# First loads of a streaming encoder: x tiles 0 to 2 by ScalarE's queue, norm rows in one transfer, small tables behind x, a third place for turned tiles

## The reference

```
for layer in (0, 1):
    h = rms_norm(x, pre_mix_g[layer])
    y = even_mixer(h) if layer == 0 else gla_mixer(h)
    x = x + rms_norm(y, post_mix_g[layer])
    h = rms_norm(x, pre_ffn_g[layer])
    x = x + rms_norm((silu(h @ w_gate) * (h @ w_up)) @ w_down, post_ffn_g[layer])
```

## Time and profile before

| what | before |
|---|---|
| median of the runs | 1456.67 us (1454.84 to 1458.1) |
| profiled execution | 1451.34 us, its span 1449.5 us |
| busy share: TensorE, VectorE, ScalarE, GpSimd | 96%, 57%, 37%, 27% |
| mean granted TensorE clock | 0.989 of 2.4 GHz |
| moved by DMA | 131.49 MB, mean 91 GB/s |

### The profile page before, as it was taken

One profiled execution on the slowest core, in us unless ns is written; L12 is line 12 of the kernel. 1 busy time (PEld: TensorE's weight loads), 2 busy tenths in 40 slices (PEclk: granted clock), 3 DMA queues, 4 the chain that ended last, 5 costly groups with the idle time before them and its releaser, 6 DMA issues.

```text
span 1449.5 us, 20838 instructions
## 1 busy us (share of the span) xinstructions
PE 1384.4 (96%) x9097; PEld 1313.3 (91%) x9097; DVE 823.7 (57%) x928; ACT 530.4 (37%) x740; POOL 390.2 (27%) x307
## 2 busy tenths in 40 slices
PE   5999989999999999988999999998999999999996
PEld 5998979999999999987899877997979898999996
DVE  4447376765655556458343454647686565555744
ACT  5223243442433334334333213424344243433444
POOL 2042051433324233114001100005143332424304
PEclk9999999999999999988999999999999999999998
DMA  6221204122122212322232321420412212222231
GB/s 213 88 88 45 88 29 160 59 87 89 59 88 88 88 59 87 123 89 102 88 124 81 110 94 59 151 83 30 160 58 88 88 59 91 84 88 87 88 117 73
DMA packets 92144, 131.49 MB, mean 91 GB/s; under 512 B 2631, under 2 KB 76179, under 8 KB 91286
## 3 DMA queue, kind: packets, MB, share of 16 engines
q1 hardware_dynamic: 87832, 110.21, 23.3%
q0 software_dynamic: 3808, 19.42, 3.8%
q10 hardware_dynamic: 414, 0.54, 0.1%
HBM read 114.42 MB, written 15.74 MB: 90 GB/s over the span
## 4 chain that ended last, share of the span: by engine, by line
PE 77%; DVE 13%; ACT 4%; issue 3%; POOL 2%; DMA 1%; ACTq 0%; SPq 0%; DVEq 0%; POOLq 0%
PE ps L550 25%; PE ps L541 19%; PE ps L631 5%; PE ps L586 5%; PE ps L1053 4%; PE ps L798 4%; PE ps L783 4%; PE ps L741 4%; DVE wl L1114 2%; PE ps L666 1%; DVE wl L1249 1%; PE ps L683 1%; PE ps L1026 1%; POOL x L2094 1%; PE ps L1039 1%
## 5 line engine op out<-in xcount | busy, mean ns | idle before, releaser
L1114 DVE TENSOR_TENSOR wl<-stage,wh 128x2048 fp32r<-128x2048 f32 x57 | 140.3, 2462 | 79.5 <-ACT wh L1734 44.5
L1725 ACT ACTIVATE wh<-stage 128x2048 fp32r<-128x2048 f32 x47 | 89.7, 1907 | 179.3 <-PE ps L541 119.8
L2164 POOL TENSOR_TENSOR wsum<-stage 128x512 f32<-128x512 f32 x36 | 46.7, 1296 | 401.8 <-DVE wl L1249 250.5
L1249 DVE TENSOR_TENSOR wl<-wsum,wh 128x2048 fp32r<-128x2048 f32 x36 | 82.5, 2290 | 30.1 <-ACT wh L1754 29.8
L541 PE MATMUL ps<-xh,wh 128*128 128x320 f32 x352 | 80.5, 310 | 3.9 <-DVE qk L1120 2.4
L1803 ACT ACTIVATE gate<-ps 128x320 f32<-128x320 f32 x72 | 31.3, 435 | 143.0 <-PE ps L550 143.0
L1242 DVE TENSOR_TENSOR wbl<-stage,wbh 128x1024 fp32r<-128x1024 f32 x36 | 44.4, 1233 | 67.0 <-ACT wbh L1744 67.0
L541 PE MATMUL ps<-xh,wl 128*128 128x320 f32 x352 | 80.2, 309 | 0.0
L541 PE MATMUL ps<-xl,wh 128*128 128x320 f32 x352 | 80.1, 309 | 0.0
L586 PE MATMUL ps<-wh,xh 128*128 128x256 f32 x240 | 68.1, 284 | 0.0
L586 PE MATMUL ps<-wh,xl 128*128 128x256 f32 x240 | 67.9, 283 | 0.0
(11 more groups left out here) (365 smaller groups left out, 4485.4 us busy)
## 6 DMA issues: line engine op xcount, KB each, us to landing
stage<-w_ffn_gate SPq DMA_DIRECT2D x22, 1024.0 KB, 5.3
stage<-w_ffn_up SPq DMA_DIRECT2D x22, 1024.0 KB, 5.3
stage<-w_ffn_down SPq DMA_DIRECT2D x22, 1024.0 KB, 5.1
stage<-w_in_odd SPq DMA_DIRECT2D x12, 1024.0 KB, 5.3
x_spill<-x POOLq DMA_DIRECT2D x3, 2560.0 KB, 8.5
x<-x_spill SPq DMA_DIRECT2D x3, 2560.0 KB, 10.5
stage<-w_in_even SPq DMA_DIRECT2D x6, 1024.0 KB, 5.0
stage<-w_out_even SPq DMA_DIRECT2D x4, 1024.0 KB, 5.5
```

The costliest lines, as they stand in the source:

```text
L1114: dve.tensor_tensor(wl[:, s].rearrange("p k c -> p (k c)"), stage[:, s, :], f32(wh[:, s].rearrange("p k c -> p (k c)")), ALU.subtract).the ...
L1249: dve.tensor_tensor(wsl[:, u % 2, :], wsum[:].rearrange("p i c -> p (i c)"), f32(wsh[:, u % 2, :]), ALU.subtract).then_inc(w_lo, 1)
L1725: act.activation(wsh[:, u % 2, :], flat_stage(u), ACT.Copy).then_inc(w_hi, 1)
```

## The change

The norm rows are put together on the host into one array of 76 rows of 128 and come in one transfer. ScalarE's own queue issues x tiles 0, 1 and 2 as its first instructions; SP issues the identity, the rows, weight unit 0, x tiles 3 and 4, then weight unit 1. GpSimd waits until x tile 4 has landed before it issues its 13 small loads. Turned tile 2 gets a place of its own, banks 1 and 3 (free until the second half of unit 0); tiles 3 and 4 then wait for tiles 0 and 1 only, and the second half of unit 0 waits until tile 2 has been copied. VectorE's and ScalarE's orders are written out: VectorE gain 0, gain 1, low 0, gain 2, low 1, low 2, gain 3, `lo(0)`, gain 4, low 3, low 4; ScalarE high 0, copy 0, high 1, copy 1, high 2, `hi(0)`, copy 2 (in two halves), then high and copy of tiles 3 and 4.

```diff
+        def x0_banks(t):
+            b = (4, 6, 0, 4, 6)[t]
+            return ps[:, 0:4, :].rearrange("p (i b) n -> p i b n", b=2)[:, :, 1, :] if t == 2 else ps[:, b:b + 2, :]
+        def x0_tiles(t):
+            return x0_banks(t).rearrange("p b (k n) -> p b k n", n=P)
...
-            r0 = 0
-            for name in ("pre_mix_g", "post_mix_g", "pre_ffn_g", "post_ffn_g", "pool_scale", "g_onorm"):
-                src = a[name].rearrange("l (k p) -> (l k) p", p=P)
-                sp.dma_start(rows[r0:r0 + src.shape[0], :], src).then_inc(rows_loads, 16)
-                r0 += src.shape[0]
-            for t in range(TT):
-                src = a["x_prompt"][0, tile(t), :] if t < 4 else a["x_sample"].rearrange("b s d -> (b s) d")
-                sp.dma_start(xin[:, t, :], src).then_inc(x_load[t], 16)
-                if t == 0:
-                    load(0, a["w_in_even"][0, :, 0:UW], wait=False)
+            sp.dma_start(rows[0:ROWS, :], a["rows"]).then_inc(rows_loads, 16)
+            load(0, a["w_in_even"][0, :, 0:UW], wait=False)
+            sp.dma_start(xin[:, 3, :], a["x_prompt"][0, tile(3), :]).then_inc(x_load[3], 16)
+            sp.dma_start(xin[:, 4, :], a["x_sample"].rearrange("b s d -> (b s) d")).then_inc(x_load[4], 16)
...
                 pe.wait_ge(x_load[t], 16)
-                if t >= 2:
-                    pe.wait_ge(x0_done, t - 1)
-                    pe.wait_ge(xg_done, t - 1)
+                if t >= 3:
+                    pe.wait_ge(x0_done, t - 2)
+                    pe.wait_ge(xg_done, t - 2)
                 for k in range(KB):
-                    last = pe.transpose(span(4 + 2 * (t % 2), D)[:, tile(k)], xin[:, t, tile(k)], ident)
+                    last = pe.transpose(x0_tiles(t)[:, k // 4, k % 4, :], xin[:, t, tile(k)], ident)
...
             pe.wait_ge(x0_lo, TT)
+            pe.wait_ge(x0_done, 3)
             first_unit(1).then_inc(w_used, 1)
...
+            x0_gained(0)
+            x0_gained(1)
+            x0_low(0)
+            x0_gained(2)
+            x0_low(1)
+            x0_low(2)
+            x0_gained(3)
+            lo(0)
+            x0_gained(4)
+            x0_low(3)
             x0_low(TT - 1)
...
+            for t in range(3):
+                act.dma_start(xin[:, t, :], a["x_prompt"][0, tile(t), :]).then_inc(x_load[t], 16)
...
+                if t == 2:
+                    for b in range(2):
+                        last = act.activation(x[:, 4 * b:4 * b + 4, tile(t)], x0_tiles(t)[:, b], ACT.Copy)
+                    last.then_inc(x0_done, 1)
...
+            x0_high(0)
+            x0_copy(0)
+            x0_high(1)
+            x0_copy(1)
+            x0_high(2)
+            hi(0)
+            for t in range(2, TT):
+                if t > 2:
+                    x0_high(t)
+                x0_copy(t)
...
+            pool.wait_ge(x_load[4], 16)
             pool.dma_start(cst[:, P:], a["consts"][:, P:]).then_inc(small_loads, 16)
```

More of the change, by code:

```diff
@@ L484, in _ @@
             sp.dma_start(ident, a["consts"][:, 0:P]).then_inc(ident_load, 16)
-            r0 = 0
-            for name in ("pre_mix_g", "post_mix_g", "pre_ffn_g", "post_ffn_g", "pool_scale", "g_onorm"):
-                src = a[name].rearrange("l (k p) -> (l k) p", p=P)
-                sp.dma_start(rows[r0:r0 + src.shape[0], :], src).then_inc(rows_loads, 16)
-                r0 += src.shape[0]
-            assert r0 == ROWS
-            for t in range(TT):
-                src = a["x_prompt"][0, tile(t), :] if t < 4 else a["x_sample"].rearrange("b s d -> (b s) d")
-                sp.dma_start(xin[:, t, :], src).then_inc(x_load[t], 16)
-                if t == 0:
-                    load(0, a["w_in_even"][0, :, 0:UW], wait=False)
+            sp.dma_start(rows[0:ROWS, :], a["rows"]).then_inc(rows_loads, 16)
+            load(0, a["w_in_even"][0, :, 0:UW], wait=False)
+            sp.dma_start(xin[:, 3, :], a["x_prompt"][0, tile(3), :]).then_inc(x_load[3], 16)
+            sp.dma_start(xin[:, 4, :], a["x_sample"].rearrange("b s d -> (b s) d")).then_inc(x_load[4], 16)
             for u in range(1, U_OUT0):
@@ L822, in _ @@
             pe.wait_ge(ident_load, 16)
-            pe.wait_ge(rows_loads, 16 * 6)
+            pe.wait_ge(rows_loads, 16)
             pe.transpose(ps[:, 0, 0:ROWS], rows[0:ROWS, :], ident[0:ROWS, 0:ROWS]).then_inc(rows_full, 1)
@@ L1480, in x0_low, with x0_gained @@
                 dve.tensor_tensor(xl[:, :, tile(t)], xg[:, t % 2], f32(xh[:, :, tile(t)]), ALU.subtract).then_inc(x0_lo, 1)
-            for t in range(TT):
+            def x0_gained(t):
                 dve.wait_ge(x0_full, t + 1)
@@ L1485, in _ @@
                     dve.wait_ge(x0_lo, t - 1)
[L1486 to L1491, removed]
+                dve.tensor_tensor(xg[:, t % 2].rearrange("p (b k) n -> p b k n", b=2), x0_tiles(t),
+                                  gains[:, PRE_MIX:PRE_MIX + KB].rearrange("p (b k) -> p b k", b=2).unsqueeze(3).broadcast_to([P, 2, 4, P]), ALU.mult).then_inc(xg_done, 1)
+            x0_gained(0)
[8 more added lines that the diff above has]
+            x0_low(3)
             x0_low(TT - 1)
@@ L1926, in last_ffn, with x0_high, x0_copy @@
                 first_columns(TT - 1)
-            for t in range(TT):
+            for t in range(3):
+                act.dma_start(xin[:, t, :], a["x_prompt"][0, tile(t), :]).then_inc(x_load[t], 16)
+            def x0_high(t):
                 act.wait_ge(xg_done, t + 1)
                 act.activation(xh[:, :, tile(t)], xg[:, t % 2], ACT.Copy).then_inc(x0_hi, 1)
+            def x0_copy(t):
                 act.wait_ge(x0_full, t + 1)
-                act.activation(x[:, :, tile(t)], span(4 + 2 * (t % 2), D).rearrange("p (k n) -> p k n", n=P), ACT.Copy).then_inc(x0_done, 1)
-                if t == 0:
-                    hi(0)
+                if t == 2:
+                    for b in range(2):
+                        last = act.activation(x[:, 4 * b:4 * b + 4, tile(t)], x0_tiles(t)[:, b], ACT.Copy)
+                    last.then_inc(x0_done, 1)
+                else:
+                    act.activation(x[:, :, tile(t)].rearrange("p (b k) n -> p b k n", b=2), x0_tiles(t), ACT.Copy).then_inc(x0_done, 1)
+            x0_high(0)
[8 more added lines that the diff above has]
+                x0_copy(t)
             for t in range(TT):
@@ L2270 @@
     arrays["consts"] = constants()
+    arrays["rows"] = np.concatenate([arrays[name].reshape(-1, P) for name in ("pre_mix_g", "post_mix_g", "pre_ffn_g", "post_ffn_g", "pool_scale", "g_onorm")])
     aps = {name: nc.dram_tensor(name, x.shape, mybir.dt.from_np(x.dtype), kind="ExternalInput").ap() for name, x in arrays.items()}
```

## The result

| what | before | after |
|---|---|---|
| median of six runs each | 1457.38 us (1454.84 to 1460.04) | 1444.76 us (1442.83 to 1446.89) |
| ratio, 95% interval | | 0.9915 [0.9899, 0.9931] |
| profiled execution, its span | 1451.34, 1449.5 us | 1442.83, 1440.3 us |
| unit 1 starts (profiled execution) | 40.01 us | 31.94 us |

The changed kernel is 12.4 us faster by the ratio, where 7.0 was forecast; 1444.76 lies under the forecast range. The direction and the place were right, the size was not. Between the two profiled executions the span differs by 9.2 us and the start of unit 1 by 8.07.

What follows compares the result with a forecast made beforehand. TensorE, 96% busy, bounds the kernel; unit 1's start hangs on x tile 2. Landing at 10.3, plus 6.8, plus 15.87 puts unit 1 at 33.0 instead of 40.01: 7.0 us off 1456.67 gives 1449.7 us, range 1446.0 to 1454.0.

Steps and rivals of the forecast that it cites:

- How the numbers follow: Whole kernel: 7.0 us comes off the profiled execution (1451.34 to 1444.3) and off the median alike (1456.67 to 1449.7).
- Issue order on ScalarE: Kernel start: ScalarE's DMA issues go ahead of the table load, at 0.75, 1.2 and 1.65 us.
- Tile 2 lands at L = 10.3: First loads: x shares bandwidth half each with SP's queue, so x tile 2 lands at 10.3 us, called L.
- x gets more than half: Rival, 12%, first loads: tile 2 lands at 7.8, unit 1 starts at 30.4, gain 9.6 us, 1447.1 us.
- Unit 0 at L + 6.2, unit 1 at L + 22.7: First product: unit 0 can start 6.2 us after tile 2 lands, unit 1 22.7 after, at 33.0.
- From lo(0) to unit 1, 15.87: VectorE's low part of the weights to unit 1: 15.87 us, kept as one unchanged term.
- TensorE ready 1.1 before unit 1: Ahead of unit 1: TensorE is ready at 31.9 us, so the norm chain still ends last, by 1.1.
- GpSimd's wait costs nothing: GpSimd's 13 issues after tile 4 end at 21.2; its norm power, wanted at 28.7, has 7.5 us of cover.
- GpSimd held by VectorE: Part of a 17% rival: GpSimd's issues wait for busy VectorE, end at 31.5, power 2.8 late, gain 4.2, 1452.5 us.
- Only the issue time is won: Rival, 8%, first loads: tile 2 lands at 14.4, unit 1 starts at 37.1, gain 2.9 us, 1453.8 us.
- Slower by the array's rate: Rival, 5%, unit 0 on TensorE: half rate costs 2.35 us more per pass; with all six, 1462.7 us.
- Cost nothing, cover little: Norm rows in one transfer: there by 5.6 us, 4.4 after issue as upper bound, needed at about 6.6.

Runs made afterwards that it cites:

- before_again: The kernel before, unchanged, run again: 1456.46 us (12 runs); unit 1 at 42.36 us in its profiled execution.
- after_again: The changed kernel, unchanged, run again: 1444.73 us (6 runs), ratio 0.9918 to the kernel before; unit 1 at 31.66 us.
- after_late: The changed kernel with 80 unread products of the tile of ones between unit 0 and unit 1 on TensorE: 1459.70 us.
- before_c: The kernel before, unchanged, run for one more profiled execution: unit 1 at 42.10 us, 1410.0 us from there to the end.

## Why the prediction came out too small

**The step that failed** is in "How the numbers follow": "the sum is of differences inside the span, so it goes off either". It took 40.01 us, the start of unit 1 in one execution, as the kernel's own, and so also L = 17.36 for tile 2. That execution took 1451.34 us where the runs' median was 1456.67; I noted the distance and did not ask where it lay. About 2.4 us of it lay in the stretch that the change removes: typical is 42.4 (the median of the six is 42.35).

**The sum with what was measured.** Forecast 7.0; the new start 1.1 earlier than forecast (31.9 for 33.0); the old start 2.4 later: 10.5. The spans of the profiled executions say the same (means 1452.5 of six and 1442.0 of three, 10.5). The medians differ by 11.6 to 12.6, the means of all runs with a clock on record by 11.2, runs at equal clock by 10.4 to 11.6. So about 1 us between the starts and the runs stays open, no more than the uncertainty: the mean of six starts of before is itself known to 0.9 to either side. A smaller share of half-rate time in the changed kernel, which I had expected for the rest, is not needed and not shown: runs at or under 0.984 are 27 of 70 before and 3 of 13 after, and the difference stays when the clock is equal.

**The new start, by its steps.**
- *Issue order on ScalarE*: right. DMA issues at 0.75, table load at 2.15 behind them.
- *Tile 2 lands at L = 10.3*: too late, it landed at 8.6. Half each against the weights was right: 0.62 MB against 0.56 from 5.2 to 8.3, with three packets of SP for one of x, not one for one. Mis-sized was the time that x has alone. SP's queue held the identity and the rows ahead of the weight unit, 204 packets of 512 B; from 3.5 to 5.0 x moved 0.57 MB of 0.61. I had counted 0.33 MB ahead of the sharing. The rival "x gets more than half" gave L = 7.8 and a start of 30.4 for another reason; neither L nor start was reached. Tiles 3 and 4 came at 12.0 and 13.3, some 0.5 later than forecast, so the turns were not back to back; turn 3 waited 1.81 us.
- *Unit 0 at L + 6.2, unit 1 at L + 22.7*: with 8.6 that is 31.3, measured 31.94. The 0.6 lie on VectorE: gain 2 stands behind low 0 in the new order and starts at 11.45, 1.25 after turn 2 has ended at 10.20. With tile 2 earlier, the engines bound the stretch and not the landing.
- *From lo(0) to unit 1, 15.87*: exact in the changed kernel. In before it holds only where the array is at its full rate: in before_again it is 42.36 - 25.46 = 16.90.
- *TensorE ready 1.1 before unit 1*: 0.8. *GpSimd's wait costs nothing*: right, with 5.57 us to spare for 7.5.
- *GpSimd held by VectorE*: refuted, the issues took 8.49 us.
- *Only the issue time is won*: refuted. Here the rule of the Trainium skill, DMA: Bandwidth & Descriptors, "Issuing engines are not separate DMA queues", has to be read with care: the engines are shared as it says, but without ScalarE's queue the median is 3.1 us over. A second queue also changes what stands ahead of what: tile 1 no longer waits for a whole weight unit.
- *Slower by the array's rate*: no cost seen; the first pass took 2.42 us in all three executions of the changed kernel. The mechanism was real, but mostly on the other side: it delays the first pass of the kernel before by 0.6 to 1.7 us in four executions of six. The changed kernel touches it: in after_again the granted clock was at half (0.50, 1.2 GHz) from 12 to 15, and turns 3 and 4 took the half rate; in after_late, the same code up to there, the first pass took 2.64. From the TensorE timeline of after_again:

```profile
12.20 3.33 PE L835 MATMUL ps<-cst,xin 128*128 128x128 f32 x16 [2.11 <-DMA xin<-x_prompt]
```

**The prices of the rows' one transfer and of the wait.** "Cost nothing, cover little" for the rows took 4.4 us as an upper bound from the old kernel. As six transfers beside x by ScalarE's queue they would need 4.8 from the last issue and hold turn 0 until 8.52; as one it is there at 5.17 and still releases the first turn, just as tile 0 has landed. The one transfer is part of the gain, not free tidying.

## What to carry to other kernels

Before pricing a change from one profiled execution, compare its own time with the median of the runs and ask how much of the distance may lie in the stretch that the change touches; here the start that waited for transfers spread over 3.3 us, the other over 0.4. At this cold start the second queue paid by the order of the bytes and not by more bandwidth: what the first product needs goes first, tables of later layers wait, and a second queue keeps a large transfer from standing whole ahead of urgent ones. Early data shows its worth only with an order on the engines that can take it: loads alone gave 6.8 us, order alone 1.8, both 11.6.

## What the runs showed of the hardware

- The granted clock column does not show the low rate of the array with which an execution begins: in all executions here it shows 1.00 (2.4 GHz) from the first microsecond, while eight transposes take 1.97 us, and later 1.07; in before_again it shows 1.00 even beside the first pass of 4.26 us. It does show a later fall: 0.50 at 25 and 26 in before_c, where turn 4 takes 1.94 after a turn 3 of 1.07. At the start the durations of equal matmuls are the better gauge. TensorE had done nothing but transposes, with gaps of up to 3.5 us, when the rate rose in the earlier trace rows.
- Transfers from one execution to the next: tile 2 of the same kernel was turned between 17.40 and 19.62, tile 1 between 14.55 and 17.86. The changed kernel's turn 2 started within 0.25 us in three.
- Two hardware queues shared the engines by bytes, not by packets, while both had large transfers (0.62 MB in 180 packets against 0.56 MB in 542); small packets of 512 B went about one for two of 4 KB (87 against 156), so that a queue that begins with small ones gets little.
- A product of two float32 tiles of 128 by 128 is two matmuls in the trace, some 0.22 us at the full rate (18.03 us for 80), where a transpose of a float32 block takes 1.07 / 8 = 0.13 us.
